# Gate rows of a two-block transformer kernel: made by a store of the modulation columns to DRAM and a broadcast load, in place of products of all-ones with diagonals on TensorE

## What is computed

```
c_act = silu(c)                                   # c: one vector of 1024
for i in range(2):
    mod = c_act @ w_ada[i] + b_ada[i]             # 6 x 1024 numbers
    sh1, sc1, g1, sh2, sc2, g2 = split(mod, 6)
    h = rmsnorm(x, norm_mix_g[i]) * (1 + sc1) + sh1
    m = fourier_mixer(h) if i == 0 else retention_mixer(h)
    x = x + g1 * m                                # g1, g2: one number a channel, the same for all tokens
    h = rmsnorm(x, norm_ffn_g[i]) * (1 + sc2) + sh2
    x = x + g2 * swiglu(h)
out = rmsnorm(x, final_norm_g) * (1 + scf) + shf
```

## Time and profile before

| | |
|---|---|
| time, median of 3 runs (range) | 1172.46 us (1171.18 to 1173.0) |
| profiled execution | 1173.02 us |
| its span | 1170.1 us |
| PE, PEld | 98%, 83% of the span |
| DVE, ACT, POOL | 71%, 46%, 2% |
| DMA | 259.81 MB, mean 222 GB/s |
| granted TensorE clock | 0.994 of full |

### The profile page before, as it was taken

The page is one execution under the profiler, slowest core; times in us unless marked ns, Lnnn a source line. Parts: engine busy times, 40 slices in busy tenths (PEclk is TensorE's granted clock), DMA queues, the critical chain, the costliest instruction groups (busy, mean ns, idle before and its releaser), DMA issues.

```text
span 1170.1 us, 14019 instructions
## 1 busy us (share of the span) xinstructions
PE 1145.0 (98%) x5840; PEld 966.8 (83%) x5840; DVE 835.0 (71%) x957; ACT 539.3 (46%) x521; POOL 27.5 (2%) x51
## 2 busy tenths in 40 slices
PE   6999999999999999999999999999999999999997
PEld 5998898888788888888788888879976887888886
DVE  4789987987666767567656767478955866767655
ACT  5566656643544444456463434344422435434432
POOL 1000000000000000000000000000001000000000
PEclk8999999999999999999999999999999999999999
DMA  7763463438447778542447687458753564786761
GB/s 289 298 227 144 167 265 135 154 144 304 169 176 293 268 274 315 214 145 96 159 178 294 257 309 290 189 186 318 289 199 123 204 263 144 258 304 260 295 247 38
DMA packets 38638, 259.81 MB, mean 222 GB/s; under 512 B 4144, under 2 KB 6448, under 8 KB 7856
## 3 DMA queue, kind: packets, MB, share of 16 engines
q1 hardware_dynamic: 36960, 251.84, 58.1%
q0 software_dynamic: 1616, 7.08, 1.7%
HBM read 257.86 MB, written 1.05 MB: 221 GB/s over the span
## 4 chain that ended last, share of the span: by engine, by line
PE 83%; DVE 9%; DMA 3%; issue 2%; ACT 2%; POOL 1%; SPq 0%; POOLq 0%; ACTq 0%; DVEq 0%
PE pair L428 42%; PE pair L493 20%; PE pair L454 7%; PE pair L509 4%; DVE w_lo L1196 4%; PE tp L550 3%; PE tp L612 2%; DMA raw<-stream 2%; DMA mskf<-masks 1%; PE tp L785 1%; PE pair L724 1%; PE tp L713 1%; ACT w_hi L816 1%; PE tp L639 1%; PE tp L763 1%
## 5 line engine op out<-in xcount | busy, mean ns | idle before, releaser
L1196 DVE TENSOR_TENSOR w_lo<-raw,w_hi 128x2048 fp32r<-128x2048 f32 x182 | 413.3, 2287 | 91.6 <-ACT w_hi L816 91.0
L816 ACT ACTIVATE w_hi<-raw 128x2048 fp32r<-128x2048 f32 x182 | 347.4, 1915 | 226.3 <-DMA raw<-stream 143.0
L428 PE MATMUL pair<-w_hi,ht_lo 128*128 128x512 f32 x816 | 326.5, 400 | 14.1 <-DVE w_lo L1196 14.1
L428 PE MATMUL pair<-w_lo,ht_hi 128*128 128x512 f32 x816 | 319.2, 391 | 0.0
L428 PE MATMUL pair<-w_hi,ht_hi 128*128 128x512 f32 x816 | 318.9, 391 | 0.0
L428 PEld LDWEIGHTS pair<-w_hi,ht_lo 128*128 128x128 f32 x816 | 154.0, 189 | 47.8 <-DVE w_lo L1196 16.0
L428 PEld LDWEIGHTS pair<-w_lo,ht_hi 128*128 128x128 f32 x816 | 153.8, 188 | 32.9
L428 PEld LDWEIGHTS pair<-w_hi,ht_hi 128*128 128x128 f32 x816 | 154.2, 189 | 31.4 <-issue 1.2
L1205 DVE SCALAR_TENSOR_TENSOR raw<-raw,crow 128x1024 f32<-128x1024 f32 x112 | 132.3, 1218 | 0.8 <-DMA raw<-stream 0.8
L493 PE MATMUL pair<-w_hi,gt_lo 128*128 128x512 f32 x272 | 107.3, 395 | 0.3 <-DVE gt_lo L1268 0.3
L493 PE MATMUL pair<-w_lo,gt_hi 128*128 128x512 f32 x272 | 106.0, 390 | 0.0
(11 more groups left out here) (221 smaller groups left out, 1251.5 us busy)
## 6 DMA issues: line engine op xcount, KB each, us to landing
raw<-stream SPq DMA_DIRECT2D x238, 1024.0 KB, 4.9
xres<-x SPq DMA_DIRECT2D x2, 512.0 KB, 6.7
prow<-rows POOLq DMA_DIRECT2D x1, 1024.0 KB, 10.3
xres<-x POOLq DMA_DIRECT2D x2, 512.0 KB, 4.8
dt<-decay POOLq DMA_DIRECT2D x1, 1024.0 KB, 6.9
outT<-outb SPq DMA_DIRECT2D x4, 256.0 KB, 2.3
csr<-dft POOLq DMA_DIRECT2D x1, 768.0 KB, 4.3
crow<-rows POOLq DMA_DIRECT2D x1, 512.0 KB, 6.7
```

The source lines that it names most:

```text
L428: mm = pe.matmul(pair[use % 2][:, t, :], a[:, 4 * c + k, t * P:(t + 1) * P], b[:, w % WS, k * 512:(k + 1) * 512], start=(c == 0 and k == 0 ...
L816: sc.activation(w_hi[:, w % WS, :], raw[:, n % RAW, :], ACT.Copy).then_inc(hi_done, 1)
L1196: v.tensor_tensor(w_lo[:, w % WS, :], raw[:, n % RAW, :], whi32[:, w % WS, :], ALU.subtract).then_inc(raw_done, 1)
```

## The change

The diagonals, the products of all-ones and the copies go, with their PSUM jobs. In their place VectorE adds the bias to the eight columns of a gate and counts up `gate_cols`. POOL waits for that, stores the columns to a DRAM tensor `gates` of 4 x 1024 so that channel 128 m + p comes to place 128 m + p, waits for the store, and loads that row into all 128 partitions of `grow`. The gated add waits for this load (`row_in`).

```diff
+            def gate_row(n):
+                at = (16, 40, 64, 88)[n]
+                pool.wait_ge(gate_cols, n + 1)
+                pool.dma_start(gates[n].rearrange("(m p) -> p m", p=P), mod[:, at:at + 8], allow_slow_non_contiguous=True).then_inc(gate_out, 16)
+                pool.wait_ge(gate_out, 16 * n + 16)
+                pool.dma_start(grow[n % 2][:], gates[n:n + 1, :].to_broadcast([P, D])).then_inc(row_in, 16)
...
             rsqrt(RQ["mix"], 4)
+            gate_row(0)
             rsqrt(RQ["ffn"], 2)
             pool.wait_ge(w_used, W0["down0"] + GROUPS)
             pool.dma_start(csr[:], dft).then_inc(dft_in, 16)
             rsqrt(RQ["norm2"], 2)
             rsqrt(RQ["norm3"], 2)
-            pool.wait_ge(tp_done, JOB["rows1"] + 2)
+            gate_row(1)
+            pool.wait_ge(tp_done, JOB["h1"] + GROUPS)
             pool.dma_start(dt[:], decay).then_inc(decay_in, 16)
             pool.dma_start(rt[:], rot).then_inc(rot_in, 16)
             rsqrt(RQ["norm4"], 2)
+            gate_row(2)
             rsqrt(RQ["av"], 8)
             rsqrt(RQ["norm5"], 2)
+            gate_row(3)
             rsqrt(RQ["norm6"], 2)
...
             tokens("dft1", 0, (2, 3))
-            gate_rows("rows0", 1)
             wait_split("norm2b", 2)
...
-            down("down1", "h1", after={(4, 1): lambda: gate_rows("rows1", 2),
-                                       (GROUPS - 3, 1): turn_tile("norm4", xn, 0, xn_done, 9)})
+            down("down1", "h1", after={(GROUPS - 3, 1): turn_tile("norm4", xn, 0, xn_done, 9)})
...
-            gate_rows("rows2", 3, dgb)
...
-            down("down2", "h2", after={(4, 1): lambda: gate_rows("rows3", 4)},
+            down("down2", "h2", after={},
...
-                dve.wait_ge(sem("row_copied"), rows)
+                dve.wait_ge(row_in, 8 * rows)
...
+            def gate_columns(n, used):
+                at = (16, 40, 64, 88)[n]
+                dve.wait_ge(raw_done, AT_RAW["a", used - 1] + 1)
+                v.tensor_tensor(mod[:, at:at + 8], mod[:, at:at + 8], colv("b_ada", at, 8), ALU.add).then_inc(gate_cols, 1)
...
-                    mod_columns(0, 24, 18)
+                    mod_columns(0, 16, 18)
                     mod_scale(0, 8, colv("mix_g", 0, 8))
-                    gate_diagonals(16)
+                    gate_columns(0, 12)
...
-                    mod_columns(40, 48, 30)
-                    gate_diagonals(40, JOB["rows0"] + 2)
+                    gate_columns(1, 24)
...
-            mod_columns(64, 72, 37)
-            gate_diagonals(64, None, dgb)
+            gate_columns(2, 36)
...
-            mod_columns(88, 96, 53)
-            gate_diagonals(88)
+            gate_columns(3, 48)
```

More of the change, by code:

```diff
@@ L124, in plan_psum @@
              ("norm2", 2, "norm"), ("dft1", 4, "split"),
-             ("norm2b", 2, "norm"), ("rows0", 2, "row_copied"), ("dft1b", 4, "split"),
-             ("norm3", 4, "norm"), ("h1", GROUPS, "split"), ("rows1", 2, "row_copied"),
-             ("norm4", 4, "norm"), ("sc", 4, "sc_read"), ("rows2", 2, "row_copied"),
+             ("norm2b", 2, "norm"), ("dft1b", 4, "split"),
+             ("norm3", 4, "norm"), ("h1", GROUPS, "split"),
+             ("norm4", 4, "norm"), ("sc", 4, "sc_read"),
              ("av", 8, "av_read"), ("ty", 8, "split"), ("norm5", 4, "norm"),
-             ("h2", GROUPS, "split"), ("rows3", 2, "row_copied"), ("norm6", 4, "fin_read")]
+             ("h2", GROUPS, "split"), ("norm6", 4, "fin_read")]
     for name, n, kind in table:
@@ L166, with program @@
     for t in range(k))}
-def program(nc, stream, x, pT, cols, rows, sg_wT, masks, ident, dft, rot, decay, outT):
+def program(nc, gates, stream, x, pT, cols, rows, sg_wT, masks, ident, dft, rot, decay, outT):
     with ExitStack() as ctx:
@@ L227, in program @@
         pt = [sb("pt_hi", 195.25, [P, 2, S], F32R), sb("pt_lo", 197.25, [P, 2, S], F32R)]
-        dg = sb("dg", 88, [P, KT, P])
-        dgb = sb("dgb", 185.25, [P, KT, P])
         prod = sb("prod", 92, [P, 2, TT, 256])
@@ L310, in program @@
         cs_done = sem("cs_done")
-        dg_done = sem("dg_done")
+        gate_cols = sem("gate_cols")
+        gate_out = sem("gate_out")
+        row_in = sem("row_in")
         rot_done = sem("rot_done")
@@ L564, in wait_split @@
                 pe.wait_ge(lo_done, SPLIT[JOB[name]] + n)
[L566 to L573, removed]
             def hidden(name, jobs, j):
@@ L939, in _two @@
                 return a.rearrange("p (a b) -> p a b", a=2)
[L941 to L945, removed]
             norm_squares(RQ["norm0"], 0, 0)
@@ L1095, in _ @@
                 norm_his("norm2", t, moda[:, 0, :], mod[:, 0:8])
-            gate_rows("rows0", grow[0])
             dft_his("dft1b", 1, (0, 1, 2))
@@ L1113, in _ @@
             for w in range(W0["down1"], W0["down1"] + GROUPS - 4):
-                if w == W0["down1"] + 4:
-                    gate_rows("rows1", grow[1])
                 tick(w)
@@ L1138, in head_his @@
                     turned(JOB["ty"] + 2 * hd + t, gt, hd, t)
-            gate_rows("rows2", grow[0])
             for gr in range(4):
@@ L1158, in _ @@
             for w in range(W0["down2"], W0["down2"] + GROUPS - 1):
-                if w == W0["down2"] + 3:
-                    gate_rows("rows3", grow[1])
                 tick(w)
@@ L1305, in mod_scale @@
                                             op0=ALU.add, op1=ALU.mult))
[L1307 to L1312, removed]
             def hidden_los(jobs, j):
@@ L1851 @@
     args.append(nc.dram_tensor("outT", (KT, P, S), F32, kind="ExternalOutput").ap())
-    program(nc, *args)
+    gates = nc.dram_tensor("gates", (4, D), F32, kind="Internal").ap()
+    program(nc, gates, *args)
     r = run_bass_kernel_spmd(nc, [arrays], core_ids=[0])
```

## The result

The kernel after takes 1177.89 us in the median of 13 runs (1173.28 to 1181.35); the one before, run beside it, 1172.89 (1170.95 to 1174.03, 13 runs). The ratio is 1.0044, with a 95% interval of 1.0033 to 1.0054: it is slower by 5.0 us. 1167.3 was forecast, and the range ended at 1170.9. The profiled execution took 1180.11 us, 2.2 above that median, so the times in the trace add up to more than 5.0.

What follows compares the result with a forecast made beforehand. TensorE was taken to bound the kernel (busy 98%, 83% of the chain). Gains of 0 + 1.72 + 1.72 + 1.72 = 5.16 us, added costs 0, gave 1167.3 us; own range 1166.3 to 1168.3, towards B to 1170.9.

Steps and rivals of the forecast that it cites:

- What is removed: TensorE's all-ones products for four gate rows, 1.72 us each, were to give 5.16 us; hidden VectorE and ScalarE work gives 0.
- rows 1 to 3: Gate rows in down1, before rg and in down2: removing their products was to give 1.72 us each, together 5.16.
- row 0: Gate row in the Fourier mixer: gain 0, since TensorE would wait until 539.21 for VectorE's ht_lo.
- Rival A: All four gate rows pay, the Fourier mixer's too: 6.88 us gained, 1165.6 us; chance 0.08.
- The trip and its cover: POOL's store, broadcast and issues take 12.5 us, at most 34.2, within covers of 35.4 to 37.9 us; cost 0.
- Rival D: The store and broadcast take over 38 us, so gated adds wait for row_in: 1177 us for 43; chance 0.02.
- Traffic: 2.1 MB more on 259.8 makes the weight stream about 2.5 us late per row, against 12.0 slack: cost 0.
- rival C: The 1024 small pieces hold up the weight stream, 6.8 us lost in each of four stages: 1194 us; chance 0.05.
- Rival B: Stream or a block boundary swallows the shift, only one row of three pays: 1170.7 us; chance 0.12.

## Why the prediction was wrong

- **What is removed: held.** 5.16 us were forecast for rows 1 to 3 and nothing for row 0. Without the store 5.7 are gained, and the wait of 1.6 us for ht_lo stands in the Fourier mixer in place of row 0's products. Rival A, all four rows, is out.
- **The trip and its cover: held, though the trip was longer.** Store, broadcast and issues come to 11.7 + 9.8 + 0.9 + 0.6 = 23.0 us, where 12.5 were taken and 34.2 was the bound. It stays inside the covers of 35 to 38 us; the gated adds are released by TensorE. Rival D is out. But the estimate of 4.6 for the store, twice outT, was off by 7: outT's 32 pieces an engine have 512 B each, and their landing said nothing on what a piece of 4 B takes.
- **Traffic: the step that failed, twice.** "Cost 0, at worst a microsecond or two" counted the bytes of the broadcast and not the time in which the store holds the engines. This time was in rival C, with 0.29 us a piece as its upper price. Measured are 0.13, below the 0.19 from which C was to decide, and yet C's mechanism is what happened. Of its two signs one came, TensorE's waits for w_lo inside the down stages; the other, a landing over 20 us, did not (11.7). So its threshold was wrong, that is, the slack. I had read 12.0 us at chunk 5 of `down1` and used it for every place. But the last four chunks of an output product are run for tile 0 one behind the other, 2.73 us each instead of 5.45, and use up the lead.

  The last w_lo of `down0`, `down1` and `down2` before, in VectorE's timeline (start, us):

```profile
475.34 2.29 DVE L1196 TENSOR_TENSOR w_lo<-raw,w_hi 128x2048 fp32r<-128x2048 f32 x1 [0.97 <-ACT w_hi L816]
...
742.95 2.29 DVE L1196 TENSOR_TENSOR w_lo<-raw,w_hi 128x2048 fp32r<-128x2048 f32 x1 [3.15 <-ACT w_hi L816]
...
1141.09 2.29 DVE L1196 TENSOR_TENSOR w_lo<-raw,w_hi 128x2048 fp32r<-128x2048 f32 x1 [0.37 <-ACT w_hi L816]
```

  And where TensorE stopped for one after, in its timeline:

```profile
485.43 0.76 PE L505 MATMUL pair<-w_hi,gt_lo 128*128 128x512 f32 x1 [3.44 <-DVE w_lo L1183]
...
753.55 0.47 PE L505 MATMUL pair<-w_hi,gt_lo 128*128 128x512 f32 x1 [1.83 <-DVE w_lo L1183]
...
1153.56 0.47 PE L521 MATMUL pair<-w_hi,gt_lo 128*128 128x512 f32 x1 [1.10 <-DVE w_lo L1183]
```

  And the first product of the last chunk of each stage before:

```profile
481.18 0.39 PE L493 MATMUL pair<-w_hi,gt_lo 128*128 128x512 f32 x1
...
748.91 0.39 PE L493 MATMUL pair<-w_hi,gt_lo 128*128 128x512 f32 x1
...
1145.85 0.39 PE L509 MATMUL pair<-w_hi,gt_lo 128*128 128x512 f32 x1
```

  In `down0` the low part was ready at 475.34 + 2.29 = 477.63 and wanted at 481.18: slack 3.6 us. In `down1` it is 748.91 - 745.24 = 3.7, in `down2` 1145.85 - 1143.38 = 2.5. (After, `down1` stopped at the last chunk but one, the other two at the last.) Against a halt of 8 to 9 us these are little, and what catches up afterwards is slow, since a chunk passes in 4.8 (DMA) + 1.9 (ScalarE) + 2.3 (VectorE) = 9.0 us through three slots.
- **Not in the prediction at all: the clock.** A wait of 3.4 us was followed by 13 products at 1.2 GHz, 2.7 us more; one of 1.8 us by 1.6 us more. Waits of 1.1 and 0.7 us in `down2` were followed by none. The length of the wait alone doesn't decide it: with the stores on ScalarE TensorE waited 2.0 us in `down2`, until 1150.44, and the clock stayed full,

```profile
1150.00:1155.00 5.00, 4.56 (x20) 3.84 (x21) 4.88 (x6) 0.37 (x1) 0.00 (x0) 1.00 0.01 3
```

  and behind its wait of 3.4 us in `down0` the low clock cost 1.7 us and not 2.7. What decides was not tried.
- **Rival B** (the shift is swallowed) named the thin place of `down2`, 2.75 us, and a delay by the broadcast. The place was thin, the cause another: the broadcast delays nothing in the kernel without the store.

The Trainium skill (DMA: Bandwidth & Descriptors, Queues, rings and completion order) says that an engine alternates between queues by whole packets, and that a packet holds at most 64 descriptors, about 9 to 17 as a rule. I had weighed this rule against C. One could turn it round and say that the 64 pieces of an engine stood in one packet and kept the stream out. The experiment with ScalarE speaks against that: with 1040 packets a store the stream falls to 36 GB/s, with 32 to 38 GB/s. So taking turns by packets didn't protect the stream, and big packets aren't what stopped it. The traces show that the stream's own packets stay open for 4.0 us in place of 0.34; what the engine does meanwhile no run shows.

Two things remain. The store costs 5.3 us with the rows on TensorE and 10.6 without them, where the sum of the parts would have both the same. Matched product by product, the trace with the store alone loses 6.4 us in `down0`, 1.2 in `down1` and nothing in `down2`, the one of after 7.1, 3.6 and 2.2. So most of the difference lies where TensorE comes 1.72 us earlier to the last chunks and has so much less slack (a wait of 0.7 against 1.8 us in `down1`, and no low clock there; none against 1.8 in `down2`). 1.72 would about cover these waits, but another part can be the broadcast, which follows each store while the stream catches up. It costs nothing without the store; no run has the halt with and without it at the same slack, so this stays open.

And the later first store gave back 4 to 5 us by the medians, where its stage had lost 7.1. The traces differ by 1177.8 - 1171.2 = 6.6, as the profiled execution of after was 2.2 above its median and the other at its own. In them `down0` gives back all 7.1, and `down1` loses 4.6 instead of 3.6 (a wait of 2.2 us instead of 1.8, and the low clock again).

## What to carry to other kernels

Count a DMA by its pieces, not its bytes: a store of 4 KB in 1024 pieces held up all DMA engines, and a stream beside it missed two 1 MB chunks. Before a halt of a stream is priced, read the slack at the chunk that is needed soonest, often the last of a stage where the order of the work changes, and not at the one beside the edit; then add that the clock can cost nearly as much again after a wait of about 2 us and more. If columns have to become a row through DRAM, turn them on VectorE first: 32 pieces of 128 B kept the whole gain.

## What the runs showed of the hardware

- Landing of 4 KB from 128 partitions: 4.3 us in 128 pieces, 5.6 in 256, 7.2 in 512, 11.0 to 12.8 in 1024 (medians of three kernels), and 3.3 for each of four stores of 8 pieces of 128 B. From ScalarE's queue 1024 pieces took 13.3.
- While the 1024 pieces are under way another queue's stream falls from 284 to 38 GB/s for eight microseconds, and the engines are counted as fully busy. The time is booked to the stream's packets (some 4.0 us each, 0.34 before), not to the store's. It is the same with 32 packets a store (GpSimd's queue, 38 GB/s) and with 1040 (ScalarE's, 36 GB/s).
- The granted clock was 0.50 for 5.7 us after TensorE had waited 3.4 us, and 0.58 for 3.9 us after 1.8. After a wait of 2.0 us in another kernel it stayed 1.00.
